# The second mixer's projections in the order keys, values, queries, and its rotations partly inside the attention

## The chip, the cores and the metric

One core of a Trainium2 chip runs one program. The metric is the device time of an execution in microseconds (us). TensorE multiplies, ScalarE and VectorE read its results from PSUM (8 banks of 128 x 512 fp32) and prepare its operands, SyncE and GpSimd issue DMAs. The engines run their own instruction streams and meet only at semaphores.

## The reference, cut to what matters

Two transformer-like blocks of two layers each on 256 tokens of width 1024, all in fp32. The change lies in layer 1 of the first block, whose mixer is a sliding-window attention with 16 query heads on 4 key/value heads, over the 256 tokens and the 256 tokens of a context:

```python
pl = u_lat @ w; pc = u_ctx @ w            # w: 1024 x (1024 + 256 + 256)
ql, kl, vl = pl[..., :D], pl[..., D:D + kvw], pl[..., D + kvw:]
ql, kl = rms_norm(ql, q_gain), rms_norm(kl, k_gain)   # over 64 of a head
kc, vc = rms_norm(pc[..., D:D + kvw], k_gain), pc[..., D + kvw:]
ql, kl = apply_axial_rope(ql, cos, sin), apply_axial_rope(kl, cos, sin)
s = concat(ql @ kl.T (window |i - j| <= 128), ql @ kc.T, sink)
y = softmax(s)[..., :-1] @ concat(vl, vc)
h_lat = h_lat + ga1 * (y @ wo)
```

The rotation needs, for each group of 32 rows of a head, its two halves of 16 exchanged: out = x * cos + exchanged(x) * sin.

## The kernel before, in words

Activations lie transposed: 1024 features as 8 row blocks of 128 partitions, tokens along the free dimension (256, or 512 with the context). Every fp32 product is made of three fp32r products: a weight and an activation are each split into a high and a low half (w_hi, w_lo; u_hi, u_lo), and hi*hi, hi*lo, lo*hi are added in PSUM (`products`, L730 to L732; for values L800 to L802). Weights arrive in units of 128 x 1024 through a ring of four (`raw`, `w_hi`, `w_lo`); ScalarE writes the high half (`split_unit`, L1144), VectorE the low half (`lower`, L1576), three units ahead of TensorE. A unit's slot in the ring is written again when TensorE is done with the unit four places earlier. The order of the weights in DRAM is the order in which the stages use them.

A stage is a row of tiles (`make_plan`). For a query or key tile (kind QK) TensorE makes 24 products into one of four banks (`TILE`); ScalarE squares it (L1160), VectorE copies it to SBUF (L1618); one tile later, between two products, TensorE sums the squares of each head with a block of ones (`sum_tile`, L818); ScalarE takes the root in four instructions (`qk_root`, L1274, L1148, L1149, L1276); VectorE scales (`qk_scale`, L1770 to L1772). ScalarE and VectorE take these steps in the fixed order of their streams: in each turn of `stage`, first the weight half of a unit three ahead, then the square or copy of this tile, then root or scale of the tile before; the last tile of a body of four has its root or scale at the end of the body. Values (kind V) are made with tokens on the partitions, two units for 256 columns, into two banks at a time.

The stages around the change: down0b (end of the first layer), a norm of the rows with modulation (`norm`, "mix1") which releases u_hi and u_lo row block by row block, q1 (8 tiles of 256 columns, tokens only), k1 (2 tiles of 512 columns, tokens and context), v1 (2 units), the attention ATT1, and wo1 (output projection). The stage behind a norm works by row blocks (`first_tiles`): its first three tiles advance together as the norm releases blocks. SyncE loads weight units in order, each as soon as its slot's low half is made.

Rotation: GpSimd waits for four scaled tiles, copies them by DMA with the halves exchanged into `turned` (eight DMAs for a batch, L2352), in three batches: q1 tiles 0 to 3, 4 to 7, then k1. VectorE rotates a tile in three instructions (`rope`, L1758 to L1760: sine product, cosine product, sum), two tiles behind each of the first three tiles of k1 and v1 and four behind the last, all before the attention. TensorE waits for all ten ahead of the attention (L973).

The attention goes through 16 groups, each of two heads and 128 queries against 512 keys. For group n TensorE makes scores (L914), VectorE adds the window and takes the maximum (`att_max`, L2120 to L2128), ScalarE the exponentials and their sums (`att_exp`, L1440), VectorE divides (`att_scale`, L2136 to L2140), TensorE transposes (L925), ScalarE copies the transposed (`att_probs_t`, L1427), TensorE multiplies with the values (L940), ScalarE and VectorE write the high and low half of an output for every second group (L1448, L2148). TensorE's order is scores n+1, transposes n-1, values n-2; VectorE's is maximum n, scale n-1, low half n-3. Scores alternate between banks 0, 1 and 2, 3; transposes use banks 4, 5, outputs 6 and 7.

## Time and profile before

| | |
|---|---|
| median of 3 runs | 1714.46 us (1712.07, 1714.46, 1714.72) |
| span of the profiled execution, first to last instruction | 1706.6 us |
| busy: TensorE (PE), VectorE (DVE), ScalarE (ACT), GpSimd (POOL) | 94%, 77%, 51%, 6% of the span |
| mean granted TensorE clock | 0.982 |
| q1, k1, v1 on TensorE | 704.28 to 765.5 us of the span |
| first scores of ATT1, first product of wo1 | 771.91, 834.99 us |

The profiled execution has no time of its own beside the three runs, only its span; the median lies 7.9 us above it. Matmuls overlap in the pipeline, so a row's duration is longer than its pitch to the next. "issue" in a view is time in which an engine waited for nothing that the profile shows.

### The profile page before, as it was taken

How to read it: one execution, taken by the hardware profiler on the slowest of the kernel's cores; microseconds unless marked ns; L12 is line 12 of the kernel's file. 1: busy time of each engine (PE TensorE's matmuls, PEld its weight loads, DVE VectorE, ACT ScalarE, POOL GpSimd, SP SyncE). 2: the span in 40 equal slices, each digit the busy share in tenths (PEclk: the TensorE clock that was granted, in tenths of full speed). 3: DMA queues.
4: the chain of work that ended last, by engine and by line, in shares of the span. 5: the costliest groups of instructions: out<-in, count | busy, mean ns of one | idle time of the engine just before them, and what ended most of it. 6: DMA issues, size and time to landing. Idle time of an engine off the chain costs nothing.

```text
span 1706.6 us, 32698 instructions
## 1 busy us (share of the span) xinstructions
PE 1606.4 (94%) x11872; PEld 1421.1 (83%) x11872; DVE 1308.7 (77%) x2229; ACT 869.5 (51%) x1505; POOL 104.3 (6%) x174
## 2 busy tenths in 40 slices
PE   6999899899999999788989999889999999899999
PEld 3778666688888888674789999789999998699999
DVE  5899897788767867678677787777887686578874
ACT  4664386343213433566555555355555586555542
POOL 0001030000000023120000212000000000000000
PEclk9999999999999999998999999999999999999999
DMA  9246651345667855340156667735555644055554
GB/s 368 89 137 224 218 149 51 123 144 184 202 193 238 263 173 169 112 140 12 53 186 202 217 208 263 316 102 176 179 183 177 205 153 158 13 164 183 182 196 137
DMA packets 80828, 292.02 MB, mean 171 GB/s; under 512 B 10432, under 2 KB 12224, under 8 KB 78928
## 3 DMA queue, kind: packets, MB, share of 16 engines
q1 hardware_dynamic: 69552, 249.03, 44.4%
q0 software_dynamic: 11168, 41.54, 7.6%
q8 instruction: 69, 1.13, 0.3%
q14 instruction: 39, 0.32, 0.1%
HBM read 270.54 MB, written 18.68 MB: 169 GB/s over the span
## 4 chain that ended last, share of the span: by engine, by line
PE 73%; DVE 18%; issue 4%; ACT 3%; DMA 2%; ACTq 0%; DVEq 0%; SPq 0%; POOLq 0%
PE bank L730 22%; PE bank L732 21%; PE bank L731 21%; DVE stat L2121 2%; DVE w_lo L1576 2%; DVE prob L2140 1%; PE bank L914 1%; DVE bank L1588 1%; DVE ada_raw L1589 1%; PE bank L925 1%; DMA raw<-weights 1%; PE bank L940 1%; DVE qk L1771 1%; DMA ada_raw<-ada_w 1%; PE bank L818 1%
## 5 line engine op out<-in xcount | busy, mean ns | idle before, releaser
L730 PE MATMUL bank<-u_hi,w_hi 128*128 128x256 f32 (+1 forms) x1936 | 615.9, 318 | 31.2 <-DVE u_lo L1951 19.2
L731 PE MATMUL bank<-u_lo,w_hi 128*128 128x256 f32 (+1 forms) x1936 | 600.8, 310 | 0.0
L732 PE MATMUL bank<-u_hi,w_lo 128*128 128x256 f32 (+1 forms) x1936 | 600.8, 310 | 0.0
L1576 DVE TENSOR_TENSOR w_lo<-raw,w_hi 128x1024 fp32r<-128x1024 f32 x372 | 452.2, 1222 | 143.9 <-ACT w_hi L1144 131.4
L1144 ACT ACTIVATE w_hi<-raw 128x1024 fp32r<-128x1024 f32 x360 | 375.4, 1049 | 172.8 <-PE bank L732 142.7
L730 PEld LDWEIGHTS bank<-u_hi,w_hi 128*128 128x128 f32 x1936 | 372.5, 192 | 59.6 <-issue 35.7
L731 PEld LDWEIGHTS bank<-u_lo,w_hi 128*128 128x128 f32 x1936 | 372.8, 193 | 22.3 <-issue 3.8
L732 PEld LDWEIGHTS bank<-u_hi,w_lo 128*128 128x128 f32 x1936 | 372.6, 192 | 18.4
L730 PE MATMUL bank<-hid_hi,w_hi 128*128 128x512 f32 (+1 forms) x512 | 174.0, 340 | 0.0
L732 PE MATMUL bank<-hid_hi,w_lo 128*128 128x512 f32 (+1 forms) x512 | 172.1, 336 | 0.0
L731 PE MATMUL bank<-hid_lo,w_hi 128*128 128x512 f32 (+1 forms) x512 | 172.0, 336 | 0.0
L730 PEld LDWEIGHTS bank<-hid_hi,w_hi 128*128 128x128 f32 x512 | 97.1, 190 | 11.0 <-issue 1.5
L732 PEld LDWEIGHTS bank<-hid_hi,w_lo 128*128 128x128 f32 x512 | 97.1, 190 | 10.2
L731 PEld LDWEIGHTS bank<-hid_lo,w_hi 128*128 128x128 f32 x512 | 97.1, 190 | 9.7
L1589 DVE SCALAR_TENSOR_TENSOR ada_raw<-ada_raw,silu_row 128x1024 f32<-128x1024 f32 x80 | 97.7, 1222 | 9.3 <-DMA ada_raw<-ada_w 9.0
L730 PE MATMUL bank<-f_hi,w_hi 128*128 128x256 f32 x352 | 99.8, 283 | 0.0
L731 PE MATMUL bank<-f_lo,w_hi 128*128 128x256 f32 x352 | 99.6, 283 | 0.0
L732 PE MATMUL bank<-f_hi,w_lo 128*128 128x256 f32 x352 | 99.6, 283 | 0.0
L1195 ACT ACTIVATE rs<-bank 128x512 f32<-128x512 f32 (+1 forms) x64 | 31.3, 489 | 125.2 <-PE bank L732 118.7
L730 PEld LDWEIGHTS bank<-f_hi,w_hi 128*128 128x128 f32 x352 | 67.6, 192 | 0.2
L732 PEld LDWEIGHTS bank<-f_hi,w_lo 128*128 128x128 f32 x352 | 67.6, 192 | 0.0
L731 PEld LDWEIGHTS bank<-f_lo,w_hi 128*128 128x128 f32 x352 | 67.6, 192 | 0.0
(317 smaller groups left out, 2260.3 us busy)
## 6 DMA issues: line engine op xcount, KB each, us to landing
raw<-weights SPq DMA_DIRECT2D x372, 512.0 KB, 3.4
ada_raw<-ada_w SPq DMA_DIRECT2D x80, 512.0 KB, 4.1
ada_first<-ada_w SPq DMA_DIRECT2D x16, 512.0 KB, 14.4
bias_sb<-bias_na POOLq DMA_DIRECT2D x16, 256.0 KB, 3.4
toep_dram<-zeros POOLq DMA_DIRECT2D x8, 512.0 KB, 9.1
bat_dram<-bat POOLq DMA_DIRECT2D x16, 256.0 KB, 4.2
ca_dram<-ca POOLq DMA_DIRECT2D x16, 256.0 KB, 3.8
s_bat<-bat_dram POOLq DMA_DIRECT2D x4, 1024.0 KB, 8.2
```

The costliest lines, as they stand in the source:

```text
L730: pe.matmul(dst, wh, hi[:, kt, xs], start=first, stop=False)
L731: pe.matmul(dst, wh, lo[:, kt, xs], start=False, stop=False)
L732: return pe.matmul(dst, wl, hi[:, kt, xs], start=False, stop=final)
L818: pe.matmul(SUM_BANKS[b2][:, 0:s.tok], C("block"), sq[:, b2, 0:s.tok], start=True, stop=True).then_inc(S["p2"], 1)
L914: pe.matmul(psum[2 * (g % 2) + a][:, 0:keys], q_ap, k_ap, start=True, stop=True).then_inc(att_s, 1)
L925: mm = pe.transpose(psum[4 + a][:, t * P:(t + 1) * P], prob[:, 2 * (g % 2) + a, t * P:(t + 1) * P], C("ident"))
L940: mm = pe.matmul(psum[6 + pr % 2][a * HD:(a + 1) * HD, qt * P:(qt + 1) * P], heads[a][2][t], prob_t[:, 2 * (g % 2) + a, t * P:(t + 1) * P] ...
L1144: A(w_hi[:, slot, :], raw[:, slot, :], ACT.Copy).then_inc(S["hi"], 1)
L1195: chain.link(A(rs[:, b2, 0:s.tok], bank[:, 0:s.tok], ACT.Relu))
L1576: TT(w_lo[:, slot, :], raw[:, slot, :], w_hi[:, slot, :].bitcast(F32), ALU.subtract).then_inc(S["lo"], 1)
L1589: STT(raw_, raw_, 1.0, silu_row[:, 0, :], ALU.mult, ALU.mult, accum_out=ada_acc[:, b, a % 4, 0:1]).then_inc(S["ada_read"], 1)
L2121: red = dve.tensor_reduce(stat[:, 0, b, :], both[:, :, 0:keys], AX.X, ALU.max, negate=True)
```

## The change

The weights of the second mixer are packed and used in the order keys, values, queries. k1 is now the stage behind the norm (two tiles advance together), v1 uses banks 2 and 3, and both head sums of k1 stand inside v1's first unit. q1 is unrolled on ScalarE and VectorE. The exchange goes in four batches: k1, q1 tiles 0 and 1, tiles 2 to 4, tiles 5 to 7. VectorE rotates the two keys behind q1 tile 3, query tile 0 behind tile 5 and tile 1 behind tile 6, and query tiles 2 to 7 in the attention's steps 1, 3, 5, 7, 9 and 11, between the maximum of the step and the scale of the one before. The first group's scores are issued inside q1's tile 6, once the keys and query tile 0 are rotated; its maximum follows copy and scale behind tile 7 on VectorE, its exponentials stand ahead of tile 7's root on ScalarE. Scores alternate between banks 6, 7 and 0, 1; transposes use banks 2 and 3, outputs 4 and 5. `stat`, `neg_sink` and the sine products get memory of their own.

```diff
...
         Stage("down0b", "RES", 8, units=2, tok=TOK, norm=True, gate=(0, 5)),
-        Stage("q1", "QK", 8),
         Stage("v1", "V", 2, tok=TOK),
+        Stage("q1", "QK", 8),
...
         col_y = place("col_y", [P, 4], at=rsn_at + 1056)
-        stat = place("stat", [P, 4, 4, 2], at=rsn_at)
-        neg_sink = place("neg_sink", [P, HEADS], at=rsn_at + 256)
+        stat = place("stat", [P, 4, 4, 2])
+        neg_sink = place("neg_sink", [P, HEADS])
+        rope_sin = place("rope_sin", [P, 2, SEQ], at=ada_at + 12288)
...
         bias_in = [sem(f"bias_in{i}") for i in range(4)]
-        rope_in, rope_d = [sem(f"rope_turned{n}") for n in range(3)], sem("rope_done")
+        rope_in, rope_d = [sem(f"rope_turned{n}") for n in range(4)], sem("rope_done")
...
-        WHOLE = ("win", "k2", "q2")
+        WHOLE = ("win", "q1", "k2", "q2")
         def turns(eng, s, n, chain=None, per=0, unrolled=(*TABLES, *WHOLE)):
...
-        NORM_BEFORE = {"qk0": 0, "up0a": 1, "q1": 2, "up1a": 3}
+        NORM_BEFORE = {"qk0": 0, "up0a": 1, "k1": 2, "up1a": 3}
         HANDOVER = {"v0": (("qk0", ("a1", "d1")),), "down0a": (("up0a", ("a1",)),), "up0b": (("down0a", ("d1",)),),
-                    "down0b": (("up0b", ("a1",)),), "k1": (("q1", ("a1", "d1")),),
-                    "v1": (("k1", ("a1", "d1")), ("q1", ("a1", "d1"))), "down1a": (("up1a", ("a1",)),),
+                    "down0b": (("up0b", ("a1",)),), "v1": (), "q1": (("k1", ("a1", "d1")),),
+                    "down1a": (("up1a", ("a1",)),),
+        ROPES = ((8, 9), (0, 1), (2, 3, 4), (5, 6, 7))
+        ROPE_BATCH = {m: n for n, tiles in enumerate(ROPES) for m in tiles}
+        ROPE_PLACE = {m: n for n, m in enumerate((8, 9, *range(8)))}
+        def score_pair(g):
+            return g % 2 if g < 32 else (3, 0)[g % 2]
+        def turned_pair(g):
+            return 2 if g < 32 else 1
+        def out_bank(g):
+            return psum[(6 if g < 32 else 4) + g // 2 % 2]
         MODS_NEEDED = {"mix0": 4, "mlp0": 10, "mix1": 16, "mlp1": 22}
+        def value_bank(s, pair, b):
+            return TILE[2 + b] if s.name == "v1" else TILE[pair % 2 * 2 + b]
...
-            KT_FIRST = ("qk0", "up0a", "q1", "up1a", "glu")
+            KT_FIRST = ("qk0", "up0a", "k1", "up1a", "glu")
             def lead(s):
-                return 2 if s.name == "glu" else 3
-            SUMS_BEFORE = {"v0": "qk0", "k1": "q1", "v1": "k1", "q2": "k2", "v2": "q2"}
+                return 2 if s.name in ("k1", "glu") else 3
+            SUMS_BEFORE = {"v0": "qk0", "v1": "k1", "q2": "k2", "v2": "q2"}
             def sums_inside(s, j):
...
                     prev = SUMS_BEFORE.get(s.name)
-                    return ((ST[prev], ST[prev].tiles - 1),) if prev else ()
+                    first = 0 if prev == "k1" else ST[prev].tiles - 1 if prev else 0
+                    return tuple((ST[prev], n) for n in range(first, ST[prev].tiles)) if prev else ()
...
                     bank_left(s, (s.tile0 + jj) % RING)
+                    if s.name == "q1" and j >= 2:
+                        pe.wait_ge(S["a1"], value("a1", ST["v1"], 1))
...
                             sum_tile(*sums[t // 3])
+                        if s.name == "q1" and i * body + jj == 6 and t == 5:
+                            pe.wait_ge(pre_ka, 4)
+                            att_scores(ATT1, 0, 32)
             def value_tile(s, i, jj, body):
...
                         xs = slice(tt * P, (tt + 1) * P)
-                        dst = TILE[jj // 2 % 2 * 2 + tt // 2][:, tt % 2 * VW:(tt % 2 + 1) * VW]
+                        dst = value_bank(s, jj // 2, tt // 2)[:, tt % 2 * VW:(tt % 2 + 1) * VW]
...
             def att_scores(groups, m, base):
                 g = m + base
-                if g >= 2:
+                if base and m % 2 == 0:
+                    pe.wait_ge(rope_d, ROPE_PLACE[m // 2] + 1)
+                if base and m == 1:
+                    pe.wait_ge(S["a1"], value("a1", ST["q1"], 6))
+                    pe.wait_ge(S["d1"], value("d1", ST["q1"], 6))
+                if g >= 2 and not (base and m < 2):
                     q_ap, k_ap, _ = heads[a]
-                    pe.matmul(psum[2 * (g % 2) + a][:, 0:keys], q_ap, k_ap, start=True, stop=True).then_inc(att_s, 1)
+                    pe.matmul(psum[2 * score_pair(g) + a][:, 0:keys], q_ap, k_ap, start=True, stop=True).then_inc(att_s, 1)
             def att_transpose(groups, m, base):
                 g = m + base
+                if base and m == 0:
+                    stage_end(pe, ST["q1"], ("a1", "d1"))
                     for t in range(keys // P):
-                        mm = pe.transpose(psum[4 + a][:, t * P:(t + 1) * P], prob[:, 2 * (g % 2) + a, t * P:(t + 1) * P], C("ident"))
+                        mm = pe.transpose(psum[2 * turned_pair(g) + a][:, t * P:(t + 1) * P], prob[:, 2 * (g % 2) + a, t * P:(t + 1) * P], C("ident"))
             def att_values(groups, m, base):
...
                     pe.wait_ge(S["ada_read"], ST["wo0"].base["ada_read"])
+                if base and m == 0:
+                    stage_end(pe, ST["q1"], ("a2",))
                     for a in range(2):
-                        mm = pe.matmul(psum[6 + pr % 2][a * HD:(a + 1) * HD, qt * P:(qt + 1) * P], heads[a][2][t],
+                        mm = pe.matmul(out_bank(g)[a * HD:(a + 1) * HD, qt * P:(qt + 1) * P], heads[a][2][t],
...
             def attention(groups, base):
                 n_g = len(groups)
-                att_scores(groups, 0, base)
+                if not base:
+                    att_scores(groups, 0, base)
...
             row_total("down0b"); drained("down0b")
+            gemm("k1")
+            pe.wait_ge(late_in, 16)
+            gemm("v1")
             gemm("q1")
-            pe.wait_ge(late_in, 16)
-            gemm("k1")
-            gemm("v1"); drained("v1"); drained("q1"); drained("k1")
-            pe.wait_ge(rope_d, 10)
+            sum_tile(ST["q1"], 7)
+            drained("v1"); drained("k1")
...
                         for b in range(s.tok // SEQ):
-                            src = TILE[jj // 2 % 2 * 2 + b][:, :].rearrange("p (t c) -> p t c", c=VW)
+                            src = value_bank(s, jj // 2, b)[:, :].rearrange("p (t c) -> p t c", c=VW)
...
                     elif s.kind == "QK":
+                        if s.name == "q1" and i == 1:
+                            att_exp(ATT1, 0, 32)
...
                 gs = slice(2 * (g % 2), 2 * (g % 2) + 2)
-                A(prob_t[:, gs, 0:keys], bank_pair[2][:, :, 0:keys], ACT.Copy).then_inc(att_e, 2)
+                A(prob_t[:, gs, 0:keys], bank_pair[turned_pair(g)][:, :, 0:keys], ACT.Copy).then_inc(att_e, 2)
             def att_exp(groups, m, base):
...
                         act.wait_ge(att_t, 2 * g - 3 + a)
-                    A(prob[:, 2 * (g % 2) + a, 0:keys], psum[2 * (g % 2) + a][:, 0:keys], ACT.Exp, bias=stat[:, 0, b, a:a + 1],
+                    A(prob[:, 2 * (g % 2) + a, 0:keys], psum[2 * score_pair(g) + a][:, 0:keys], ACT.Exp, bias=stat[:, 0, b, a:a + 1],
             def att_out_hi(groups, m, base):
                 _, _, hp, at0, _, qt = groups[m]
-                pr = (m + base) // 2
                     act.wait_ge(att_o, m + base + 1)
-                    A(u_hi[:, hp, at0:at0 + SEQ], psum[6 + pr % 2][:, 0:SEQ], ACT.Copy).then_inc(att_h, 1)
+                    A(u_hi[:, hp, at0:at0 + SEQ], out_bank(m + base)[:, 0:SEQ], ACT.Copy).then_inc(att_h, 1)
             def attention(groups, base):
...
                         att_out_hi(groups, n - 3, base)
-                    if n < n_g:
+                    if n < n_g and not (base and n == 0):
...
             norm(2, "mix1")
-            stage("q1"); stage("k1"); stage("v1")
+            stage("k1"); stage("v1"); stage("q1")
...
                     dst = q1[:, m, :] if m < 8 else k1[:, m - 8, 0:SEQ]
-                    dve.wait_ge(rope_in[m // 4], 16 * 8)
-                    if m >= 2:
-                        dve.wait_ge(rope_d, m - 1)
-                    link(TT(prob[:, m % 2, 0:SEQ], turned[:, m, :], C("sin"), ALU.mult))
+                    dve.wait_ge(rope_in[ROPE_BATCH[m]], 16 * 8)
+                    n = ROPE_PLACE[m]
+                    if n >= 2:
+                        dve.wait_ge(rope_d, n - 1)
+                    link(TT(rope_sin[:, n % 2, :], turned[:, m, :], C("sin"), ALU.mult))
                     link(TT(dst, dst, C("cos"), ALU.mult))
-                    TT(dst, dst, prob[:, m % 2, 0:SEQ], ALU.add).then_inc(rope_d, 1)
+                    TT(dst, dst, rope_sin[:, n % 2, :], ALU.add).then_inc(rope_d, 1)
             def qk_scale(s, i, jj, body):
...
                             lower(s.unit0 + jj + 3, i, per)
-                        if s.name == "k1":
-                            rope((range(0, 2), range(2, 4))[jj])
-                        if s.name == "v1":
-                            rope((range(4, 6), range(6, 10))[jj])
+                        if s.name == "q1":
+                            rope({3: (8, 9), 5: (0,), 6: (1,)}.get(i * body + jj, ()))
+                            if i * body + jj == 7:
+                                att_max(ATT1, 0, 32)
...
                 b = g % 4
-                both = bank_pair[g % 2]
+                both = bank_pair[score_pair(g)]
...
                     us = (slice(None), hp, slice(at0, at0 + SEQ))
-                    TT(u_lo[us], psum[6 + pr % 2][:, 0:SEQ], u_hi[us].bitcast(F32), ALU.subtract).then_inc(att_l, 1)
+                    TT(u_lo[us], out_bank(m + base)[:, 0:SEQ], u_hi[us].bitcast(F32), ALU.subtract).then_inc(att_l, 1)
             def attention(groups, base):
                 for n in range(n_g + 4):
-                    if n < n_g:
+                    if n < n_g and not (base and n == 0):
                         att_max(groups, n, base)
+                    if base and n % 2 and n // 2 + 2 < KT:
+                        rope((n // 2 + 2,))
...
             norm(2, "mix1")
+            link(TS(neg_sink[:, :], VC("sink", 0, n=HEADS), -1.0, None, ALU.mult))
+            stage("k1"); stage("v1")
+            dve.wait_ge(late_in, 16)
             stage("q1")
-            dve.wait_ge(late_in, 16)
-            stage("k1"); stage("v1")
-            link(TS(neg_sink[:, :], VC("sink", 0, n=HEADS), -1.0, None, ALU.mult))
...
             pool.dma_start(rot[:, :, :, :], rot_dram).then_inc(rot_in, 16)
-            for n, (name, done) in enumerate((("q1", 4), ("q1", 8), ("k1", 2))):
+            for n, (name, done) in enumerate((("k1", 2), ("q1", 2), ("q1", 5), ("q1", 8))):
                     p1 = p0 + 16 if p0 % 32 == 0 else p0 - 16
-                    src_ = q1[p1:p1 + 16, 4 * n:4 * n + 4, :] if n < 2 else k1[p1:p1 + 16, :, 0:SEQ]
-                    pool.dma_start(turned[p0:p0 + 16, 4 * n:4 * n + (4 if n < 2 else 2), :], src_).then_inc(rope_in[n], 16)
+                    m0, m1 = ROPES[n][0], ROPES[n][-1] + 1
+                    src_ = q1[p1:p1 + 16, m0:m1, :] if n else k1[p1:p1 + 16, :, 0:SEQ]
+                    pool.dma_start(turned[p0:p0 + 16, m0:m1, :], src_).then_inc(rope_in[n], 16)
...
     mlp(0)
-    parts += [pack_units(sw_q, 8), pack_units(sw[:, D:kv_at], 8), pack_value_units(sw[:, kv_at:]), pack_units(sw_o, 8)]
+    parts += [pack_units(sw[:, D:kv_at], 8), pack_value_units(sw[:, kv_at:]), pack_units(sw_q, 8), pack_units(sw_o, 8)]
```

## Rows read from the trace of the kernel before

**Rows 1.** Windows: stretch, length, busy (instructions) of PE, PEld, DVE, ACT, POOL; clock; DMA.
```profile
783.90:825.10 41.20, 38.56 (x341) 24.63 (x342) 38.09 (x102) 32.66 (x80) 0.00 (x0) 1.00 0.01 2
```

**Rows 2.** VectorE's timeline, attention: start, duration, line, operation, idle before.
```profile
774.10 0.43 DVE L2120 TENSOR_TENSOR bank<-bank,con 128x256 f32<-128x256 f32 x1 [2.36 <-PE bank L914]
...
776.48 0.43 DVE L2120 TENSOR_TENSOR bank<-bank,con 128x256 f32<-128x256 f32 x1 [0.23 <-issue]
...
783.94 0.43 DVE L2120 TENSOR_TENSOR bank<-bank,con 128x256 f32<-128x256 f32 x1 [0.57 <-PE bank L914]
...
794.03 0.42 DVE L2120 TENSOR_TENSOR bank<-bank,con 128x256 f32<-128x256 f32 x1
...
797.62 0.42 DVE L2120 TENSOR_TENSOR bank<-bank,con 128x256 f32<-128x256 f32 x1
...
825.10 0.42 DVE L2120 TENSOR_TENSOR bank<-bank,con 128x256 f32<-128x256 f32 x1
```

**Rows 3.** VectorE's timeline: norm's end, one query step, one rotation.
```profile
714.88 0.88 DVE L1951 SCALAR_TENSOR_TENSOR u_lo<-tmp,mod,u_hi 128x256 fp32r<-128x256 f32 x2 [0.18 <-ACT u_hi L1416]
...
722.37 1.22 DVE L1576 TENSOR_TENSOR w_lo<-raw,w_hi 128x1024 fp32r<-128x1024 f32 x1
...
725.30 1.22 DVE L1576 TENSOR_TENSOR w_lo<-raw,w_hi 128x1024 fp32r<-128x1024 f32 x1
...
756.57 0.42 DVE L1758 TENSOR_TENSOR prob<-turned,con 128x256 f32<-128x256 f32 x1
...
757.82 0.42 DVE L1758 TENSOR_TENSOR prob<-turned,con 128x256 f32<-128x256 f32 x1
```

**Rows 4.** TensorE's timeline: first product of q1, two head sums, v1, wo1.
```profile
704.28 0.55 PE L730 MATMUL bank<-u_hi,w_hi 128*128 128x256 f32 x1 [6.79 <-DVE u_lo L1951]
...
733.24 0.60 PE L818 MATMUL bank<-sq,con 128*128 128x256 f32 x2
...
736.54 0.60 PE L818 MATMUL bank<-sq,con 128*128 128x256 f32 x2
...
752.93 0.36 PE L800 MATMUL bank<-w_hi,u_hi 128*128 128x256 f32 x1 [1.72 <-DVE k L1618]
...
755.87 1.02 PE L818 MATMUL bank<-sq,con 128*128 128x512 f32 x2
...
765.24 0.28 PE L802 MATMUL bank<-w_lo,u_hi 128*128 128x256 f32 x1
...
834.99 0.38 PE L730 MATMUL bank<-u_hi,w_hi 128*128 128x256 f32 x1 [1.22 <-DVE u_lo L2148]
```

**Rows 5.** ScalarE's timeline: one query step and the first exponentials.
```profile
720.70 1.04 ACT L1144 ACTIVATE w_hi<-raw 128x1024 fp32r<-128x1024 f32 x1
...
723.63 1.04 ACT L1144 ACTIVATE w_hi<-raw 128x1024 fp32r<-128x1024 f32 x1
...
776.29 0.20 ACT L1436 ACTIVATE stat<-stat 128x2 f32<-128x2 f32 x1 [9.65 <-DVE stat L2128]
...
777.63 0.20 ACT L1440 ACTIVATION_READ_ACCUMULATOR prob<-bank,stat 128x1 f32 x1
```

**Rows 6.** TensorE's timeline where it had stood idle, and scores at full clock.
```profile
729.83 0.70 PE L818 MATMUL bank<-sq,con 128*128 128x256 f32 x2 [2.35 <-ACT sq L1160]
...
771.91 3.78 PE L914 MATMUL bank<-k,q 64*128 64x512 f32 x8 [6.39 <-DVE k L1760]
...
785.85 1.13 PE L914 MATMUL bank<-k,q 64*128 64x512 f32 x4
...
1447.81 2.93 PE L1096 MATMUL bank<-sb_r,con 128*128 128x384 f32 x4 [3.49 <-DVE sb_r L2261]
```

**Rows 7.** Busy time and granted clock (PEclk) behind the last of these (windows).
```profile
1448.00:1450.00 2.00, 2.00 (x4) 1.08 (x5) 1.58 (x2) 0.35 (x1) 0.00 (x0) 0.50 0.00 0
```

**Rows 8.** GpSimd's exchange of q1's halves: one batch's issue, and its DMAs' landing.
```profile
745.21 3.81 POOL L2352 DMA_DIRECT2D turned<-q  x8 [11.07 <-DVE q L1772]
...
DMA to landing us min/median/max: 2.1/4.2/5.6
```

## The prediction

> **What bounds the kernel now.** I read the page's busy shares first (the table above). A share over 1706 us says nothing of the one stretch that changes, so next came the chain of waits between 695 and 860 us, and then the timelines of the single engines there. In that stretch no engine rules alone. TensorE sets the pace while it multiplies (one query tile of 24 products and a head sum every 3.30 us, rows 736.54 minus 733.24 [rows 4]), but it ends its last value product at 765.5 and then stands idle 6.4 us for the rotation's last instruction on VectorE [rows 6]. From there to the first product of wo1 at 835.0 VectorE is the bound: of the 41.2 us from 783.9 to 825.1 it computes 38.1, and its instructions follow each other with only their own small gaps [rows 1]. One group costs it 3.59 us when it also makes the low half of an output and 3.27 otherwise (12 steps take 825.10 - 783.94 = 41.16 us, of which 797.62 - 794.03 is the longer kind) [rows 2]. TensorE stands beside it with 3 x 1.05 us of work for a group, so it is nearly full too but waits for VectorE.
>
> **The change, part by part.** The profiled execution's span is 1706.6 us; the three runs' median is 1714.46, that is 7.9 us above it, for what lies around the span. I treat this as fixed, work out the shift inside the span and add it to the median.
>
> The price that is sure: six of the ten rotations (query tiles 2 to 7) move into the attention. A rotation is three instructions at a pitch of 1.25 us (757.82 - 756.57) [rows 3]. 6 x 1.25 = 7.5 us come onto VectorE where it has no idle time to hide them. In the old order eight of the ten stood behind 752, partly inside waits for ScalarE; the last six and two weight splits ran exposed, behind TensorE's end.
>
> What is gained has to come from an earlier start of the attention, so I walk the three queues. Prices: a query step (weight low half, copy, scale) is 2.93 us on VectorE (725.30 - 722.37) [rows 3] and 2.93 on ScalarE (split, square, root: 723.63 - 720.70) [rows 5]; of ScalarE's step the root is 1.8 and the split 1.0. TensorE needs 2.87 for a tile without its head sum and 3.30 with it [rows 4].
>
> Keys first: the walk starts from k1 on TensorE, which opens at 704.28 at the lower clock as q1 did [rows 4]. Its pairs of 512 columns are 6 products per row block, 1.4 us at full clock, and the norm releases the last block at 715.8 [rows 3], so k1 ends at 717.6. Its two tiles are the work of four of 256 columns, where the old order had three under the norm: one tile's worth (2.9 us) more hides there. Values: 12.4 us as before (765.24 + 0.12 - 752.93) plus one more head sum of 0.9 [rows 4], until 730.9. The old 1.72 us wait ahead of v1 (from 751.2, for the keys' copy) goes, since v1 now uses the other two banks. The keys' two roots and scales are over by 729.0, under v1; VectorE idles there and nothing is late from it.
>
> Queries: tiles 0 to 4 end at 733.7, 737.0, 740.3, 743.6, 746.9. At the boundary of the two blocks of four ScalarE makes two roots in a row, as it did at 726.6, where TensorE lost 2.35 us [rows 6]; now it is less behind, the square of tile 4 is there at 748.9, and tile 5 ends at 751.2 (1.0 us lost). VectorE has scaled tile 2 at 747.5, rotates the keys until 749.9 (their exchange, asked for at 729.0, has landed), and then owes a scale, two weight halves, two copies and a scale (5.9 us) ahead of query tile 0, whose rotation ends at 757.05. Its exchanged halves: issued from 744.2 for 3.8 us, landed at most 5.6 later [rows 8], by 753.7: in time by 2 us.
>
> Now the added wait: inside tile 6 TensorE issues the first group's scores, which wait for that rotation. It gets there at 753.8 and stands 3.3 us. Queued behind it are the scores (1.1 us at full clock [rows 6]) and the last 0.7 us of tile 6, done at 758.9; the square of tile 6, root 5, copy 6 and scale 5 on ScalarE and VectorE wait for these (VectorE idle 1.3 + 1.3 us). Scale 5 ends at 762.8, rotation 1 at 764.0, then weight half, copy 7, scale 6: 766.9. First maximum 2.2 us (774.10 to ScalarE's start 776.29), first exponentials 1.5 (to 777.83) [rows 2, 5]. ScalarE does them ahead of root 7 (1.8), and VectorE's scale 7 (1.5) waits for this root: 3.3 us idle. The second group's maximum starts at 773.9; before it started at 776.48 [rows 2]. Gain 2.6 us.
>
> From there to the last group's maximum the old kernel took 48.6 us, 1.0 more than 12 steps at 41.16 and two at 3.25, because TensorE came out of its idle time at half clock (two groups' scores in 3.78 us at 771.91, against 1.13 for one at 785.85) [rows 2, 6]. The new one needs 47.6 + 7.5. It too opens cold: TensorE has 6 us of nothing between the second group's scores (764.5) and the third's (770.7) and again until the first transpose at 778.1. At half clock transposes and scores of 2.0 us each end at 782.2, where VectorE wanted them at 781.6: 0.6 us. The tail from the last maximum to wo1 (834.99 - 825.10 = 9.9 us [rows 2, 4]) keeps its order and holds no rotation.
>
> Sum: -2.6 + 7.5 - 1.0 + 0.6 = +4.5 us.
>
> **The clock in the new gap.** After an idle time of 3.49 us TensorE resumed at 0.50 of its clock, that is 1.2 of 2.4 GHz [rows 6, 7]; after 2.35 us the tiles ran on at the full pitch [rows 4, 6]. The new gap of 3.3 us lies between. If the clock falls, scores and the rest of tile 6 take 1.6 us more, and VectorE passes this on. Bounds 0 and 1.6; the 3.49 row is nearer but my gap is uncertain by more than the distance, so I take the middle, 0.8. The sum becomes +5.3 us, 1719.8 us.
> The Trainium skill, "TensorE: Matmul & The Clock Gate", section "HAM oscillation — how this bites in real kernels", says that a wait inside a run of products throttles the array again, so that each burst behind one starts cold. By that rule, which speaks against a wait in the middle of q1, the upper end holds (+6.1); by the 2.35 us row alone, the lower (+4.5).
>
> Edits at nothing: four exchange batches instead of three are 8 more issues of 0.5 us on GpSimd, idle otherwise; the moved sink negation (0.2 us) falls under the norm's wait; separate homes of stat, neg_sink and rope_sin, and other banks, change no duration. The other end for the sine buffer's chain (each rotation waits for the one two places earlier) is nil too: they are on one engine in that order. Unrolling q1 on ScalarE and VectorE could save a loop turn, below 0.1 us at 728.4.
>
> **Rivals.**
> *A better handover (not slower).* VectorE's idle 1.3, 1.3 and 3.3 us between 755 and 774 hang on one event, that TensorE is at tile 6's scores before rotation 0 is done. If VectorE is ahead there by then and ScalarE finds root 7 out of the way, 5.9 us go: the sum is -1.4, 1713.1 us. It decides once rotation 0 ends before 753.8. For it: the margin is 3.3 us, one query step. Against: VectorE shows no idle time from 744 to 757 in my walk, and ScalarE's order is fixed in the code.
> *The rotations hide in the attention.* If VectorE had 1.25 us of slack in the odd steps, the 7.5 us would vanish: -3.0, 1711.5 us. For: 3.1 of 41.2 us are not busy [rows 1]. Against: these are 0.1 us gaps between dependent instructions; only 0.6 us is a wait for TensorE.
> *The clock falls in the new gap.* The 3.49 us row repeats itself and all 1.6 us are paid: +6.1, 1720.6 us. For: the nearest row. Against: the gap may be shorter than walked, and 2.35 us cost nothing.
> *TensorE stays at half clock in the attention.* With rotations it idles 1.3 us in every pair of groups, after a start of bursts. A group is 3 x 2.0 us at half clock, 2.6 more than VectorE's 3.4; two further cold groups make +5.3, in all +11, 1725.8 us. Against: in the old kernel a run of such bursts from 777.9 on had brought the full clock back by the scores of 785.85 [rows 6].
> *The exchange comes too late*, so that the change doesn't do what it says: rotation 0 waits for its batch. The margin is 2 us; at a landing 3 us later than the slowest seen it costs 1 to 3 us: 1722 us.
>
> **How the numbers follow.** Forecast 0.34; clock falls in the gap 0.20; handover 0.20; hidden rotations 0.09; half clock 0.09; late exchange 0.08. Less than 0.2% (3.4 us) can't be told from no change here. The forecast, 1719.8, has a spread of about 3 us either way, of which a fifth falls within 3.4 us of before. The same holds for the fallen clock. So slower is 0.54 x 0.8 + 0.17 = 0.60; same takes 0.11 and most of the handover case, 0.28; faster 0.12 with the hidden rotations. The range reaches down to the handover case, 1713, and up to near the half clock's, 1725; the forecast's own is 1717 to 1723.
>
> **What would show it.** In the new profile: VectorE's maxima at pitches of about 4.5 and 3.6 us up to the twelfth group, then 3.3 and 3.6; an idle time of some 3 us on TensorE ahead of the first scores, ended by the rotation's last instruction (L1760 before); 3.3 us on VectorE ended by the root of tile 7 (L1276); the second group's maximum near 774 and wo1 near 840. I am wrong if the maxima keep a pitch of 3.4, or if the second one starts before 770, or if the granted clock reads 0.50 beyond 785.

## The result and the profile after

| | before | after |
|---|---|---|
| median of 20 runs each, same chip | 1711.12 us (1708.57 to 1716.90) | 1715.35 us (1712.87 to 1718.74) |
| ratio, 95% interval | | 1.0024 [1.0016, 1.0032] |
| span of the profiled execution | 1706.6 us | 1710.7 us |
| first product behind the norm to first product of wo1 | 130.71 us | 136.71 us |
| mean granted TensorE clock | 0.982 | 0.979 |

The change makes the kernel 0.24% slower, 4.2 us of 1711: little, but clear of the spread of the runs. A later comparison with the same two kernels gave 1.0027. The forecast was 1719.8 us.

The page of the kernel after opens with:

```profile
span 1710.7 us, 32602 instructions
PE 1606.7 (94%) x11872; PEld 1422.4 (83%) x11872; DVE 1308.1 (76%) x2229; ACT 870.1 (51%) x1505; POOL 108.6 (6%) x182
```

The lines to follow are L946 (scores, in TensorE's code), L959 (transposes), L1798 to L1800 (a rotation), L1810 to L1812 (a scale), L2160 to L2168 (the maximum of a group), L2176 to L2180 (its scale), L1314 (the end of a root). TensorE's timeline in the changed stretch, with the idle time ahead of an instruction and what ended it in brackets, answers to [rows 4, 6]:

```profile
703.73 0.76 PE L754 MATMUL bank<-u_hi,w_hi 128*128 128x512 f32 x1 [6.82 <-DVE u_lo L1991]
...
749.07 0.70 PE L845 MATMUL bank<-sq,con 128*128 128x256 f32 x2 [0.75 <-ACT sq L1198]
...
757.00 1.66 PE L946 MATMUL bank<-k,q 64*128 64x512 f32 x4 [2.87 <-DVE q L1800]
...
771.62 2.08 PE L946 MATMUL bank<-k,q 64*128 64x512 f32 x4 [5.53 <-ACT prob L1480]
...
840.44 0.38 PE L754 MATMUL bank<-u_hi,w_hi 128*128 128x256 f32 x1 [1.22 <-DVE u_lo L2188]
```

The new wait is there: 2.87 us ahead of the first group's scores, in the middle of q1, ended by the last instruction of rotation 0. VectorE's timeline of the same stretch answers to [rows 2, 3]:

```profile
756.42 0.43 DVE L1800 TENSOR_TENSOR q<-q,rope_sin 128x256 f32<-128x256 f32 x1
756.76 1.22 DVE L1615 TENSOR_TENSOR w_lo<-raw,w_hi 128x1024 fp32r<-128x1024 f32 x1
760.69 0.42 DVE L1657 COPY q<-bank 128x256 f32<-128x256 f32 x1 [2.71 <-ACT sq L1198]
762.40 0.43 DVE L1810 TENSOR_TENSOR tmp<-tmp,rsn 128x256 f32<-128x256 f32 x1 [1.29 <-ACT rsn L1314]
...
767.76 0.42 DVE L2160 TENSOR_TENSOR bank<-bank,con 128x256 f32<-128x256 f32 x1
...
773.22 0.43 DVE L1810 TENSOR_TENSOR tmp<-tmp,rsn 128x256 f32<-128x256 f32 x1 [3.32 <-ACT rsn L1314]
...
774.54 0.43 DVE L2160 TENSOR_TENSOR bank<-bank,con 128x256 f32<-128x256 f32 x1
...
787.67 0.42 DVE L2160 TENSOR_TENSOR bank<-bank,con 128x256 f32<-128x256 f32 x1
...
791.25 0.42 DVE L2160 TENSOR_TENSOR bank<-bank,con 128x256 f32<-128x256 f32 x1
...
795.78 0.43 DVE L2160 TENSOR_TENSOR bank<-bank,con 128x256 f32<-128x256 f32 x1
...
830.55 0.42 DVE L2160 TENSOR_TENSOR bank<-bank,con 128x256 f32<-128x256 f32 x1
```

VectorE waits behind the gap twice, 2.71 us for ScalarE's square of tile 6 and 1.29 us for the root of tile 5, and later 3.32 us for ScalarE's root of tile 7. The second group's maximum (774.54) comes 70.8 us behind the first product, where the kernel before needed 72.2 (776.48 - 704.28 [rows 2, 4]): 1.4 us gained. From there to the last group's maximum it is 56.0 us instead of 48.6, with the rotations visible in the pitches: 791.25 - 787.67 = 3.58 without, 795.78 - 791.25 = 4.53 with one. That costs 7.4. The rest, to wo1, is 9.9 us in both. So -1.4 + 7.4 = +6.0 us between the first product and wo1.

The windows of the kernel after (length, busy time and instructions of each engine, granted clock, DMA share, GB/s) answer to [rows 1, 7]:

```profile
787.67:830.55 42.88, 35.27 (x313) 22.47 (x312) 39.94 (x107) 29.48 (x72) 0.00 (x0) 1.00 0.01 1
757.00:759.00 2.00, 2.00 (x6) 0.71 (x7) 0.98 (x1) 0.00 (x0) 2.00 (x5) 0.61 0.68 189
759.00:761.00 2.00, 2.00 (x11) 2.00 (x11) 0.31 (x1) 0.73 (x2) 0.71 (x2) 0.53 0.87 263
```

VectorE stays the bound of the attention (39.94 of 42.88 us busy). In the four microseconds behind the 2.87 us gap TensorE's granted clock averages 0.61 and 0.53, most of the time at the lower of its two levels (1.2 of 2.4 GHz), and the scores took 1.66 us at 757.00 where they take 1.13 at full clock [rows 6].

### The profile page after: what moved, and what is told of

Read it like the earlier page. It is cut to its first block, busy times and chain, and to the rows that moved or that the text cites. A ratio compares the mean times of both kernels' runs of the same rounds, so it can differ in the third digit from the quotient of the medians.

```text
span 1710.7 us, 32602 instructions
## 1 busy us (share of the span) xinstructions
PE 1606.7 (94%) x11872; PEld 1422.4 (83%) x11872; DVE 1308.1 (76%) x2229; ACT 870.1 (51%) x1505; POOL 108.6 (6%) x182
## 3 DMA queue, kind: packets, MB, share of 16 engines
q8 instruction: 69, 1.13, 0.3%
## 4 chain that ended last, share of the span: by engine, by line
PE 73%; DVE 18%; issue 4%; ACT 3%; DMA 2%; ACTq 0%; DVEq 0%; SPq 0%; POOLq 0%
PE bank L754 22%; PE bank L756 21%; PE bank L755 21%; DVE stat L2161 2%; DVE w_lo L1615 2%; DVE prob L2180 1%; DVE bank L1627 1%; PE bank L946 1%; DVE ada_raw L1628 1%; PE bank L959 1%; DVE tmp L1810 1%; PE bank L976 1%; DVE qk L1811 1%; DMA raw<-weights 1%; PE bank L827 1%
## 5 line engine op out<-in xcount | busy, mean ns | idle before, releaser
L959 PEld LDWEIGHTS bank<-con,prob 128*128 128x128 f32 x320 | 36.2, 147 | 47.8 <-DVE prob L2180 39.7
```

The lines of the kernel that those rows point to most:

```text
L959: mm = pe.transpose(psum[2 * turned_pair(g) + a][:, t * P:(t + 1) * P], prob[:, 2 * (g % 2) + a, t * P:(t + 1) * P], C("ident"))
```

## The experiments

"Stretch" is the time from the first product behind the norm to the first of wo1, in the profiled execution: 130.71 us before, 136.71 after. Ratios are to the kernel before, timed again on the same chip in the same comparison; three chips were used, so the medians of different rows can't be subtracted from each other, the ratios can. The last column is the stretch less 136.71. The theory of all of them (A in the first texts): the rotations are paid in full in the attention; the second maximum is held by two places where one engine stands in front of what another needs, TensorE at the first scores and ScalarE at the first exponentials.

| kernel | median us (runs) | ratio [95%] | stretch us | against after |
|---|---|---|---|---|
| the change again | 1715.59 (7) | 1.0027 [1.0014, 1.0041] | 136.71 | 0 |
| root first | 1712.93 (12) | 1.0013 [1.0004, 1.0022] | 133.68 | -3.0 |
| scores late | 1711.07 (12) | 1.0002 [0.9993, 1.0011] | 132.01 | -4.7 |
| both | 1707.56 (12) | 0.9980 [0.9972, 0.9989] | 128.98 | -7.7 |
| no rotation | 1708.42 (12) | 0.9982 [0.9972, 0.9991] | 129.38 | -7.3 |
| all ahead | 1717.91 (6) | 1.0038 [1.0023, 1.0052] | 138.41 | +1.7 |
| GpSimd | 1709.40 (11) | 0.9992 [0.9982, 1.0003] | 132.21 | -4.5 |
| GpSimd and both | 1704.20 (6) | 0.9954 [0.9942, 0.9967] | 125.88 | -10.8 |
| three batches | 1720.68 (7) | 1.0045 [1.0028, 1.0062] | 142.00 | +5.3 |
| filled gap | 1714.67 (11) | 1.0013 [1.0000, 1.0026] | 134.65 | -2.1 |
| GpSimd late | 1707.97 (11) | 0.9975 [0.9964, 0.9986] | 128.69 | -8.0 |

The ratios of "scores late" and "GpSimd" can't be told from 1, nor can those of "filled gap" and the change be told from each other; for differences that small only the stretch speaks.

**The change again**, no edit.

> The changed kernel itself, unaltered, beside the kernel before on the same chip. Theory A (VectorE: 7.5 us of rotations inside a full attention against a start 1.3 to 1.9 us earlier) and theory B (the added wait in tile 6 and the half clock behind it are the whole price) both expect the first measurement again: 1.0024 of before, about +4 us.

The stretch came out the same to 0.01 us. That is one repeat, and partly luck: the end of rotation 0, ahead of all that the edits touch, lies between 52.7 and 53.2 us behind the first product in eleven executions (without "three batches", where it waits for its exchange). So a difference below half a microsecond in the stretch shows little.

**Root first.** ScalarE makes the root of tile 7 ahead of the first exponentials:

```diff
                     elif s.kind == "QK":
+                        qk_root(s, i, body - 1, body)
                         if s.name == "q1" and i == 1:
                             att_exp(ATT1, 0, 32)
-                        qk_root(s, i, body - 1, body)
```

> ScalarE makes the root of query tile 7 ahead of the first group's exponentials. Theory A: VectorE's 3.3 us idle time ahead of scale 7 (773.22 in the changed kernel) goes, the second group's maximum starts at 771.4 instead of 774.5, all behind it moves along: -3.2 us against the changed kernel, +1 against before. Theory B: the wait in tile 6 and the clock are untouched, so 0 to -0.5 us.

VectorE's timeline from the first maximum to the second:

```profile
769.33 0.42 DVE L2160 TENSOR_TENSOR bank<-bank,con 128x256 f32<-128x256 f32 x1
...
771.42 0.42 DVE L1810 TENSOR_TENSOR tmp<-tmp,rsn 128x256 f32<-128x256 f32 x1
...
772.75 0.42 DVE L2160 TENSOR_TENSOR bank<-bank,con 128x256 f32<-128x256 f32 x1
```

The 3.32 us wait is gone: the two maxima stand 3.42 us apart instead of 6.78, and the stretch is 3.0 us shorter. That wait was on the path. The missing 0.4 us lies ahead of the edit: behind the same gap of 2.87 us the granted clock stayed low until 763.8 here, in the change until 760.9, the first scores took 2.08 us instead of 1.66, and the first maximum came 64.46 us behind the first product instead of 64.03.

**Scores late.** TensorE finishes q1 before it turns to the first group's scores:

```diff
-                        if s.name == "q1" and i * body + jj == 6 and t == 5:
-                            pe.wait_ge(pre_ka, 4)
-                            att_scores(ATT1, 0, 32)
...
             gemm("q1")
             sum_tile(ST["q1"], 7)
+            pe.wait_ge(pre_ka, 4)
+            att_scores(ATT1, 0, 32)
```

> The first group's scores move from inside query tile 6 to behind the head sum of tile 7, so that TensorE never waits for a rotation inside q1 and stays at full clock to the end of q1. Theory A: the chain square 6, root 5, copy 6, scale 5, rotation 1 closes up; first maximum at 763.9 instead of 767.8, second at 770.8 instead of 774.5: -3.7 us against the changed kernel, 0 to +0.5 against before. Theory B: the whole loss goes and more, 4 to 6 us against the changed kernel.

VectorE's first maximum of this kernel, at 767.76 in the change:

```profile
764.21 0.42 DVE L2159 TENSOR_TENSOR bank<-bank,con 128x256 f32<-128x256 f32 x1
```

It comes 59.78 us behind the first product instead of 64.03. 4.7 us in all, a little more than expected: the wait and the fallen clock go together.

**Both** edits of the last two kernels.

> Both edits. Theory A: VectorE has no idle time left between rotation 0 and the second maximum, which starts at 767.5: -7.0 us against the changed kernel, so about 3 us faster than the kernel before, although the six rotations still stand in the attention. Theory B: the same as the scores moved alone.

VectorE's timeline of this kernel (in the kernels whose scores are moved, line numbers are one lower):

```profile
764.52 0.42 DVE L1811 SCALAR_TENSOR_TENSOR q<-tmp,q 128x256 f32<-128x256 f32 x1
764.87 0.42 DVE L2159 TENSOR_TENSOR bank<-bank,con 128x256 f32<-128x256 f32 x1
...
766.96 0.42 DVE L1809 TENSOR_TENSOR tmp<-tmp,rsn 128x256 f32<-128x256 f32 x1
...
768.28 0.42 DVE L2159 TENSOR_TENSOR bank<-bank,con 128x256 f32<-128x256 f32 x1
```

No bracket is left: VectorE waits for nobody between the query steps and the second maximum, which comes 63.2 us behind the first product (768.28 - 705.13) instead of 70.8. The two savings add up (3.0 + 4.7 = 7.7), and the kernel is 0.2% faster than the one before, with all six rotations still in the attention.

**No rotation.**

```diff
                     if base and n % 2 and n // 2 + 2 < KT:
-                        rope((n // 2 + 2,))
+                        dve.wait_ge(rope_in[ROPE_BATCH[n // 2 + 2]], 16 * 8)
+                        dve.nop().then_inc(rope_d, 1)
```

> The changed kernel with the rotations of query tiles 2 to 7 left out (their places in the attention only count up; the output isn't the reference's). Theory A: the attention's steps fall back from 4.5 to 3.25 us at six places: -7.5 us against the changed kernel, so 3 to 3.5 us faster than before. Rival: TensorE and ScalarE would bound the steps as well, so that only 3 to 4 us go.

The maxima of VectorE where the change has those at 791.25 and 795.78:

```profile
791.08 0.42 DVE L2160 TENSOR_TENSOR bank<-bank,con 128x256 f32<-128x256 f32 x1
...
794.42 0.42 DVE L2160 TENSOR_TENSOR bank<-bank,con 128x256 f32<-128x256 f32 x1
```

The step that held a rotation takes 3.34 us instead of 4.53. -7.3 us in all: of 7.5 us of rotations next to nothing is hidden.

**All ahead.** The six rotations in one piece between the scale of tile 7 and the second maximum:

```diff
-                    if base and n % 2 and n // 2 + 2 < KT:
-                        rope((n // 2 + 2,))
...
             stage("q1")
+            rope(range(2, 8))
             attention(ATT1, 32)
```

> The changed kernel with query tiles 2 to 7 rotated between scale 7 and the second group's maximum, none inside the attention. Theory A: the same 7.5 us of VectorE, so no gain in the attention's sum, and the last batch's exchange (issued from 774.6 for 3.9 us, landed some 4 us later) is now waited for: +4 us against the changed kernel. Rival (between the groups the rotations disturb the three engines' rhythm and cost more than their own time): 0 or less against the changed kernel.

```profile
777.87 0.43 DVE L1800 TENSOR_TENSOR q<-q,rope_sin 128x256 f32<-128x256 f32 x1
780.13 0.42 DVE L1798 TENSOR_TENSOR rope_sin<-turned,con 128x256 f32<-128x256 f32 x1 [1.84 <-DMA turned<-q]
```

+1.7 instead of +4: VectorE waits 1.84 us for the last batch, which landed 1.5 us behind its last issue, sooner than I had it. Those 1.84 us are what spreading saves (+1.7 in the stretch): it keeps VectorE from waiting for the last exchange, but it makes no rotation cheaper.

**GpSimd.** The six rotations on GpSimd, each batch behind its own exchange:

```diff
-                    if base and n % 2 and n // 2 + 2 < KT:
-                        rope((n // 2 + 2,))
...
                     pool.dma_start(turned[p0:p0 + 16, m0:m1, :], src_).then_inc(rope_in[n], 16)
+                if n >= 2:
+                    rope(ROPES[n])
```

> Query tiles 2 to 7 are rotated by GpSimd, with the same three instructions, behind its issue of the batch, instead of by VectorE in the attention. Theory A: VectorE gets its steps of 3.25 us back: -7.5 us against the changed kernel, 3 us faster than before, as long as a rotation on GpSimd takes less than 6.8 us. Rival: the two engines disturb each other in memory, VectorE's instructions grow while GpSimd computes and half or more of it is lost.

GpSimd and VectorE at the same time, first GpSimd's timeline, then VectorE's:

```profile
782.17 0.76 POOL L2393 TENSOR_TENSOR rope_sin<-turned,con 128x256 f32<-128x256 f32 x1 [1.55 <-DMA turned<-q]
...
788.91 0.73 POOL L2395 TENSOR_TENSOR q<-q,rope_sin 128x256 f32<-128x256 f32 x1
```

```profile
781.86 1.35 DVE L2180 TENSOR_SCALAR prob<-prob,stat 128x512 f32<-128x512 f32 x2
...
783.93 1.23 DVE L2161 TENSOR_REDUCE stat<-bank 128x2 f32<-128x1024 f32 x1
...
785.59 0.70 DVE L2168 TENSOR_TENSOR stat<-stat,neg_sink 128x2 f32<-128x2 f32 x1
...
786.60 1.64 DVE L2180 TENSOR_SCALAR prob<-prob,stat 128x512 f32<-128x512 f32 x2
...
790.96 0.88 DVE L2180 TENSOR_SCALAR prob<-prob,stat 128x512 f32<-128x512 f32 x2
```

4.5 of the 7.3 us came back. While GpSimd computes (782.2 to 789.6) VectorE's pair of scales takes 1.64 us; after it has ended, 0.88. The reduction out of a bank keeps its 1.23. Of the 2.8 us that are missing, 1.4 lie ahead of the second maximum (72.22 us behind the first product instead of 70.81), where GpSimd's first three rotations run beside the scale of tile 6 and the first maximum.

**GpSimd and both.** The three edits together.

> GpSimd's rotations and both edits at the attention's start (root of tile 7 ahead of the exponentials, scores behind tile 7). Theory A: the gains add up, -7.5 - 7.0 = -14 us against the changed kernel, 10 us faster than before. Rival: with the earlier start the scores of groups 2, 4 and so on wait for GpSimd's rotations, so that 3 to 6 us of it are lost.

The same stretching falls on tile 6's scale (VectorE):

```profile
763.65 1.03 DVE L1810 SCALAR_TENSOR_TENSOR q<-q,vec,rs 128x256 f32<-128x256 f32 x1
764.72 0.83 DVE L1811 SCALAR_TENSOR_TENSOR q<-tmp,q 128x256 f32<-128x256 f32 x1
```

1.03 us where the kernel after has 0.48 and 0.83 where it has 0.42. -10.8 instead of -14, and still the fastest kernel of all: 1704.2 us, ratio 0.9954.

**Three batches.** Tiles 0 to 3 in one exchange:

```diff
-        ROPES = ((8, 9), (0, 1), (2, 3, 4), (5, 6, 7))
+        ROPES = ((8, 9), (0, 1, 2, 3), (4, 5, 6, 7))
...
-            for n, (name, done) in enumerate((("k1", 2), ("q1", 2), ("q1", 5), ("q1", 8))):
+            for n, (name, done) in enumerate((("k1", 2), ("q1", 4), ("q1", 8))):
```

> The changed kernel with the exchange in three batches (the keys, query tiles 0 to 3, 4 to 7). The batch that rotation 0 needs is asked for when tile 3 is scaled (751.3 in the changed kernel) instead of tile 1 (744.2): 3.9 us of issues, about 1.6 us to land, so 756.9 against VectorE's arrival at 755.5. Theory: rotation 0 waits 1.4 us, TensorE's scores with it, and all behind moves: +1.4 us against the changed kernel. Rival: the landing takes the 4 us median of the kernel before, +3.5 to 4 us; or the wait is hidden, 0.

GpSimd's, VectorE's and TensorE's timelines, one row each:

```profile
752.54 3.86 POOL L2395 DMA_DIRECT2D turned<-q  x8 [18.14 <-DVE q L1812]
```

```profile
761.68 0.43 DVE L1798 TENSOR_TENSOR rope_sin<-turned,con 128x256 f32<-128x256 f32 x1 [5.18 <-DMA turned<-q]
```

```profile
763.17 2.08 PE L946 MATMUL bank<-k,q 64*128 64x512 f32 x4 [8.14 <-DVE q L1800]
```

The stretch grew by 5.3 us, almost exactly VectorE's 5.18 us wait; both expectations were too low, because the batch landed 5.3 us behind its last issue (752.54 + 3.86 = 756.40 to 761.68). It is the small and early batch of two tiles that keeps the exchange out of the path.

**Filled gap.** TensorE multiplies something that nobody reads while it waits:

```diff
                             pe.wait_ge(pre_ka, 4)
+                            for f in range(20):
+                                pe.matmul(psum[6][:, 0:s.tok], w_hi[:, slot, f % KT * P:(f % KT + 1) * P], u_hi[:, f % KT, 0:s.tok],
+                                          start=True, stop=True)
                             att_scores(ATT1, 0, 32)
```

> The changed kernel with 20 extra products of 256 columns into bank 6 ahead of the first scores (added work, its results are overwritten), 2.4 us, so that TensorE computes through most of its 2.9 us wait for rotation 0. Theory: the granted clock stays 1.00 from 757 to 761 instead of 0.61 and 0.53, scores and the rest of tile 6 take 2.1 instead of 3.3 us and the second group's maximum comes 1.2 us earlier: -1.2 us against the changed kernel. Rival (the low clock there is covered by other waits): 0; or the filler ends after the rotation and costs 0.5 us more.

TensorE's timeline, then the windows:

```profile
754.37 2.56 PE L807 MATMUL bank<-u_hi,w_hi 128*128 128x256 f32 x20
757.31 1.13 PE L949 MATMUL bank<-k,q 64*128 64x512 f32 x4 [0.38 <-DVE q L1803]
```

```profile
757.00:759.00 2.00, 1.69 (x9) 0.93 (x10) 1.39 (x2) 0.00 (x0) 2.00 (x5) 1.00 0.65 202
759.00:761.00 2.00, 2.00 (x17) 1.95 (x17) 0.42 (x1) 1.55 (x4) 1.11 (x3) 1.00 0.95 240
```

TensorE reaches the scores as long ahead of rotation 0's end as before, but the clock stays at 1.00 and the scores take 1.13 us. The stretch is 2.1 us shorter. Not all of that is the clock: rotation 0 ended 52.8 us behind the first product here and 53.1 in the change, and the filler can't be the reason. Counted from the end of rotation 0, the second maximum comes 16.4 us later instead of 17.7 (773.66 and 774.54 less 757.26 and 756.85): 1.3 us is what the fallen clock cost. Another 0.4 us comes in the step to the fourth maximum, which takes 3.62 us here and 4.05 in the change; that step takes between 3.55 and 4.06 us in the other kernels, so that this part is not shown to be the gap's.

**GpSimd late.** Both edits; rotations 2 to 4 stay on VectorE, 5 to 7 go to GpSimd, behind the third batch.

```diff
-                    if base and n % 2 and n // 2 + 2 < KT:
+                    if base and n in (1, 3, 5):
                         rope((n // 2 + 2,))
...
+                if n == 3:
+                    rope(ROPES[n])
```

> Both edits at the attention's start, query tiles 2 to 4 rotated by VectorE in the attention and only tiles 5 to 7 by GpSimd. Theory C (each of GpSimd's nine instructions stretches VectorE's instructions on SBUF beside it, so a rotation there gives back only part of its 1.25 us): the first three save nothing and lose nothing, the last three give 3.75 less 1.7 lost beside them: 2.1 us less than with both edits alone, about 1705.5 us. Rival (the loss comes from the exchange's DMAs and their issue, not from GpSimd's arithmetic): 3.7 us less.

GpSimd's timeline, VectorE's and TensorE's:

```profile
791.26 0.72 POOL L2396 TENSOR_TENSOR q<-q,rope_sin 128x256 f32<-128x256 f32 x1
```

```profile
792.30 1.70 DVE L2179 TENSOR_SCALAR prob<-prob,stat 128x512 f32<-128x512 f32 x2
...
798.45 0.43 DVE L2159 TENSOR_TENSOR bank<-bank,con 128x256 f32<-128x256 f32 x1 [0.87 <-PE bank L943]
```

```profile
793.19 0.66 PE L956 MATMUL bank<-con,prob 128*128 128x128 f32 x4 [1.48 <-DVE prob L2179]
...
796.65 1.73 PE L943 MATMUL bank<-k,q 64*128 64x512 f32 x4
```

128.69 against 128.98 for "both": moving three rotations away gave 0.3 us of 3.7, and both expectations were wrong. Here the two engines overlap in the attention alone. Two pairs of scales are stretched (1.72 and 1.70 us instead of 0.88) and two short instructions of the maximum between them (0.65 and 0.70 instead of 0.16), 2.7 us together; a wait for TensorE of 0.87 us gives back nearly all of the rest. That wait is the clock's: TensorE had stood 2.05 and then 1.48 us for the stretched scales, the granted clock read 0.50 from 795 to 797, and the scores took 1.73 us instead of 1.13. The rival, that the exchange's DMAs slow VectorE, falls: the last of them was issued at 771, and from 787.0 to 794.6, while GpSimd computed, the DMA engines were busy 0.01 of the time.

## Why the prediction was right and where it failed

**The step that failed is the first one, the base.** The prediction added its shift to 1714.46 us, the median of three runs, and said of the 7.9 us between the profiled span and that median: "I treat this as fixed". They are not what lies around the span. Where an execution has both its time and its span, the difference is 2.2 us (1712.93 - 1710.7 for the change itself, 1712.65 - 1710.4 for root first, 1707.44 - 1705.2 for both) and 1.8 (1709.40 - 1707.6 for GpSimd). The rest was spread: twenty runs of the kernel before, the first three among them, gave 1708.57 to 1716.90 with a median of 1711.12. The profiled execution was a quick one (1706.6 + 2.2 = 1708.8) and the three timed ones were all slower than that median. Of the miss (1719.8 - 1715.35 = 4.45 us), 1714.46 - 1711.12 = 3.3 are this base, and 1.1 the sum (+5.3 forecast, 1715.35 - 1711.12 = +4.2 measured). Against the median of twenty the forecast stood 8.7 us higher, about twice what was measured.

**The sum, term by term**, counted from the first product:

| step | predicted | measured in after |
|---|---|---|
| rotation 0 ends | 52.8 | 53.1 |
| TensorE's gap ahead of the first scores | 3.3 | 2.87 |
| idle ahead of the scale of tile 7 | 3.3 | 3.32 |
| second maximum | 69.6 (with the 0.8 of clock: 70.4) | 70.8 |
| second to last maximum | 55.7 | 56.0 |
| last maximum to wo1 | 9.9 | 9.9 |
| the stretch against before | +4.5; +5.3 with the clock | +6.0 |

*The rotations*: 7.5 us predicted, 7.3 measured by leaving them out. *The earlier second maximum*: -2.6 (-1.8 with the clock's 0.8) predicted, -1.4 measured. *The clock in the new gap*: taken at 0.8 between 0 and 1.6; it fell, and cost 1.3 by the second maximum, so the term was mis-sized by 0.5 and its bounds held. That is nearly all of what the second maximum is off. The row at 0.50 behind 3.49 us of idle time [rows 6, 7] was the one to follow. The Trainium skill, "TensorE: Matmul & The Clock Gate", section "HAM oscillation — how this bites in real kernels", says of a kernel with longer waits between its bursts that the next burst starts throttled each time; the trace shows the same behind a shorter one, with 0.61 and 0.53 behind 2.87 us. *The rest of the attention*: 55.7 predicted, 56.0 measured.

So the stretch lost 0.7 more than forecast, and yet the whole kernel lost 1.1 less. In the two profiled executions the kernel behind wo1, where nothing was changed, took 1.35 us less (span less the start of wo1: 871.61 before, 870.26 after), and the first product came 0.55 earlier. 6.0 - 1.35 - 0.55 = 4.1, the difference of the spans. That it agrees with the 4.2 us of the medians is partly luck. Over the experiments that same part took between 870.3 us (870.46 for the change again) and 878.1 ("filled gap", in one of its slowest runs), so I can't say whether the 1.35 us belong to the change. The medians show more: in all twelve comparisons the median moved by 0.5 to 3.2 us less against the kernel before than the stretch did. Either something outside the stretch is quicker in the new order, or the 130.71 us, from one quick execution, are shorter than usual. What causes it stays open; no run tests it.

Three readings of the prediction were off without entering its sum. Behind TensorE's last value product at 765.5 stood four rotations and one weight split, not six and two. Its half-clock rival adds up to +10.6 (5.3 + 5.3) or +11.4, not +11. And it counted hidden rotations, -3.0 us, as faster, though by its own 3.4 us they would have been no change.

**The rivals.** *The clock falls in the new gap* came true beside the forecast. *A better handover* was right as a mechanism and its condition was missing: rotation 0 ended at 53.1, TensorE stood at the scores 2.87 us earlier. The two edits of "both" take both waits away by another road, and then the stretch is 128.98 - 130.71 = -1.7 us against before, where the rival said -1.4. *Hidden rotations* falls by "no rotation" (7.3 us) and by the pitches (4.53 against 3.34). *Half clock in the attention*: the granted clock is 1.00 from 787.67 on, so it did not happen. *Exchange too late*: not in the change; the run with three batches shows what it would have cost, 5.3 us, more than the 1 to 3 of the text.

## What to carry to other kernels

Before work is moved off a cold stretch into a full one, look at what stands at the handover: here two orders of instructions, each an edit of a few lines, held 7.7 us, more than the six moved rotations cost. A base from three runs carries their spread: take what lies around a span from an execution that has both numbers, and ask where in the spread the few runs may lie before adding a shift smaller than it.

## What the runs showed of the hardware

**GpSimd's arithmetic slows some of VectorE's instructions.** While GpSimd computed, the TENSOR_SCALAR pair on 128x512 took 1.35 to 1.72 us instead of 0.88, SCALAR_TENSOR_TENSOR on 128x256 0.83 and 1.03 instead of 0.42 and 0.48, and a TENSOR_TENSOR of 128x2 up to 0.70 instead of 0.16. In "GpSimd late" this happened with the DMA engines nearly idle (0.01), so the exchange's transfers are not the cause. Those with an operand in a bank kept theirs (the reduction 1.23, adding the window 0.43). The Trainium skill, "GPSIMD Engine Reference", section "8. Key points", says that GpSimd shares its SBUF interfaces with VectorE and that VectorE's instructions in a 2-port mode or with two SBUF inputs contend. The trace agrees where it can be told: all that were stretched have their operands in SBUF. On GpSimd itself an instruction of a rotation took 0.72 to 0.79 us, on VectorE 0.42. Once GpSimd was the slowed one: in "GpSimd" VectorE had just begun a weight half, with two operands in SBUF, and kept its 1.22 us, while GpSimd's first instruction of a rotation took 1.56 beside it. VectorE's row, then GpSimd's:

```profile
765.23 1.22 DVE L1615 TENSOR_TENSOR w_lo<-raw,w_hi 128x1024 fp32r<-128x1024 f32 x1
```

```profile
765.47 1.56 POOL L2393 TENSOR_TENSOR rope_sin<-turned,con 128x256 f32<-128x256 f32 x1 [5.62 <-DVE q L1800]
```

**A gap of 2.87 us was enough for the granted clock to fall**, where one of 2.35 us had shown nothing [rows 6], and twenty products that nobody reads kept it at 1.00. How long it stayed low differed behind the same gap: it was back at 1.00 at 760.9 in the change and at 763.8 in "root first". And the length of one gap doesn't decide it: in "both" TensorE stood 1.69 us in every other group of the attention and the clock stayed at 1.00, in "GpSimd late" it stood 2.05 and 1.48 us within 5 us and the clock fell to 0.50.

**An exchange's landing varies by several microseconds**: 1.5 us behind the last issue where the DMA engines were busy 0.38 of the time ("all ahead", 778.6 to 780.1, three tiles), 5.3 us where it was 0.76 ("three batches", 756.4 to 761.7, four tiles, with weights on the way). Traffic and size differ together here, so which of them counts isn't shown.
